# Two cache passes of a hybrid decoder step: row loads asked for earlier in one, a fifth row buffer in the other

## The chip, the cores and the metric

The kernel runs on one core of a Trainium2 chip. The metric is the device time of one execution in microseconds (us), and the time of a version is the median of its runs. A profile is of one execution. TensorE is PE in its rows (PEld is its weight load), VectorE is DVE, ScalarE is ACT, GpSimd is POOL and SyncE is SP; SPq, ACTq and POOLq are the DMA issues of those engines. The core has 16 DMA engines that all queues share.

## The reference, cut to what matters

The program is one layer step of a hybrid autoregressive decoder: a prompt of 512 tokens and 8 sample sequences of 8 new tokens each, the latter over 4096 cached positions in pages of 128 rows. Three groups of heads share one input projection; the change lies in the sample side of the last two of them:

```
o_dsa: score = indexer(q, idx cache); keep the best 256 keys of each query (6 q / 2 kv heads)
o_cmp: attention over 32-row blocks that an MLP has compressed; its probabilities rank the 64-row blocks
o_slc: attention over the best 16 of the 64-row blocks (slc K and V of the NSA cache)
o_win: attention over the last 512 positions (window state)
nsa  = g0 * o_cmp + g1 * o_slc + g2 * o_win
```

Both `o_slc` and `o_dsa` are computed as dense passes over the whole cache with a mask for the keys that were not chosen. Each of them reads K and V of 2 heads, 8 sequences, 4096 positions, 128 wide, in float32: 64 MB, 2 MB at a time.

## The kernel before, in words

The kernel is a row of blocks, each with its own program for every engine. A block ends when all engines have come to its end; only then does the next begin. Around the change the blocks are: `compress` (TensorE-heavy), `cmp_sample` (the compressed attention), the pass `slc` over the selected blocks, the pass `dsa` over the top-k keys (called the top-k pass here), the pass `win` over the window state, and then the prompt's blocks.

The three passes are one function, `stream`. A cache pass has 32 steps: 4 groups of 2 sequences, and in each 8 pieces of 512 positions. A step needs 4 pages of each of its 2 sequences: 8 DMAs of 128 rows x 512 floats, 256 KB each, so 2 MB a step. They go into one of the row buffers: `second`, the two halves of `region`, and `rows3` (the profile calls the last one `kept_rows`). Buffer 0 is `kept_second`, buffers 1 and 2 are `kept_region`.

TensorE's program of a pass is, for each step: turn the keys of step n (`turn`, L1643), turn the probabilities of step n-1 (L1666), score step n (L1653 and L1656), and multiply the values of step n-1 (`values`, L1682), which signals `v_used`. ScalarE copies the turned keys (L1756) and does the exponentials, VectorE adds the bias with the running maximum (L1821), copies the probabilities (L1829) and adds up (L1839). In the first five steps of `slc` VectorE also does the last of the top-k search (L978, L980), and one mask (L2042).

The loads are asked for by SyncE's program, in order. In `stream` it waits for the `v_used` of the step that had the same buffer before, and then issues the 8 DMAs of the next step (L914), each with a page number that was read into a register ahead (L905). Steps below `ready` are not issued there, since an earlier block did: step 0 of `slc` in `compress`, step 1 in `cmp_sample`, behind two small loads of new values (L934) and ahead of the bias `bias_nsa` (L1013, 4 DMAs of 24 rows of 16 KB). At the end of its own steps a pass calls `ahead`: `slc` there loads half of the bias of the next pass, `kept_bias_lo` (4 DMAs of 24 rows of 8 KB and 4 of 24 rows of 32 bytes; ACT's queue brings the other half in `dsa`), and the first three steps of `dsa`; `dsa` loads the bias of `win`, its new values, and the first three of the four row sets of `win` (L1912). Each of these waits in `free(n)` until the buffer n has been used for the last time by the pass that still runs.

In `slc` VectorE first waits for `bias_nsa`, adds a mask to its end (L1581), makes the scores of the new tokens (L1804) and their maximum (L1806); ScalarE needs this for the exponentials of the new tokens (L1782), behind four copies of keys.

Of the kernel before, what the change touches and what calls it, by code (L numbers as in the profile page):

```python
# [16 lines left out]
F32 = mybir.dt.float32  # L17
# [7 lines left out]
P = 128  # L25
# [4 lines left out]
PAST = 4096  # L30
# [888 lines left out]
AHEAD = 3  # L919


def step_rows(sp, nc, io, kept, tag, cache, col, n, free):

    g, c = divmod(n, NCH)
    free(n)
    pages = page_numbers(nc, io, kept.paired, g * (2 * NPG) + c * (2 * PPC), 2 * PPC)
    for b in range(2):
        to = kept.rows[n % 4].rearrange("p (b m c) -> p b m c", b=2, m=PPC)[:, b]
        load_pages(sp, pages[b * PPC:(b + 1) * PPC], to, cache, col, 4 * DH, kept.arrived[tag][n % 4][b])


def new_values(sp, io, kept, tag, col):
# [573 lines left out]
def stream(nc, io, kept, tag, *, cache, col, heads, per, q, k_new, select=None, dropped_keys=None, bias=None,  # L1506
# [9 lines left out]
    width = heads * DH  # L1516
    items = per * heads
    acc_w = DH
    SLOTS = 4
    per_bank = CH // acc_w  # L1520
    banks = groups // per_bank
    with ExitStack() as ctx:
# [41 lines left out]

        def slot(g, c):

            return (c % SLOTS, g * (nch // SLOTS) + c // SLOTS + 1) if nch > 1 else (g % SLOTS, g // SLOTS + 1)

        def parity(g, c):
            return c % 2 if nch > 1 else g % 2  # L1570
# [12 lines left out]
        @block.sync  # L1583
        def _(sp):
            def rows_of(g):

                for c in range(nch):
                    n = c + g * nch
                    i, _ = slot(g, c)
                    if state is None and c % 2 == 0 and n + 1 >= ready:  # L1590

                        pages = page_numbers(nc, io, kept.paired, g * (2 * NPG) + c * (2 * PPC), 4 * PPC)
                    if n < ready:
                        continue
                    for b in range(per):

                        sp.wait_ge(v_used, n * per + b + 1)
                        if state is not None:
                            sp.dma_start(rows[i][:, b], state[g * per + b].rearrange("(m p) c -> p m c", p=P)).then_inc(rows_in[i][b], 64)
                        else:  # L1600
                            first = (c % 2 * per + b) * PPC
                            load_pages(sp, pages[first:first + PPC], rows[i][:, b], cache, col, 2 * width, rows_in[i][b])

            each_group(sp, rows_of)
            for to, first in extra:
                sp.wait_ge(zeroed, 3)
                load_bias(sp, io, to, first, KEYS - to.shape[1], later_in)

            def free(n):

                sp.wait_ge(v_used, SLOTS * per + (groups * nch - 4 + n + 1) * per)

            if ahead is not None:
                ahead(sp, free)
# [12 lines left out]
        def _(pe):  # L1627
            pe.nop().then_inc(k_turned, SLOTS * items)
            pe.nop().then_inc(scored, KTS)
            pe.nop().then_inc(probs_turned, 2)  # L1630
            pe.nop().then_inc(v_used, SLOTS * per)

            def turn(g, c, j):
                n = c + g * nch
# [155 lines left out]
        def _(dve):  # L1790
# [33 lines left out]
            def copy_probs(g, c):  # L1824
                n = c + g * nch
                dve.wait_ge(probs_turned, n + 3)

                dve.wait_ge(v_used, (n - 1 + SLOTS) * per)
                dve.tensor_copy(pT[parity(g, c)][:], qp[:]).then_inc(pT_copied, 1)  # L1829

            def add_up(g, c):
                n = c + g * nch
                dve.wait_ge(v_used, (n + 1 + SLOTS) * per)
                to = acc[:, bass.ds(g, 1), :].rearrange("p o c -> p (o c)")
                new = pv[parity(g, c)][:, 0:acc_w]
                dve.wait_ge(acc_done, n + 2)
                dve.wait_ge(shrunk, n + 1)
                by = shrink[:, bass.ds(g, 1), c + 1:c + 2].rearrange("p o k -> p (o k)")
                dve.scalar_tensor_tensor(to, to, by, new, ALU.mult, ALU.add).then_inc(acc_done, 1)  # L1839
# [79 lines left out]
def cmp_sample(nc, io, kept):  # L1919


    with ExitStack() as ctx:
# [17 lines left out]
        @block.sync  # L1940
        def _(sp):
            new_values(sp, io, kept, "slc", NSA_VS)
            new_values(sp, io, kept, "dsa", DSA_V)
            step_rows(sp, nc, io, kept, "slc", io.nsa_cache, 512, 1, lambda n: None)
            sp.wait_ge(bias_zeroed, 1)
            load_bias(sp, io, kept.bias_nsa, 6, 0, kept.bias_nsa_in)

        @block.gpsimd
        def _(pool):
# [72 lines left out]
def slc_sample(nc, io, kept):  # L2022
# [13 lines left out]
    def spare(dve, n):  # L2036
# [3 lines left out]
        elif n == SEARCH_LATE + 1:  # L2040
# [1 line left out]
            dve.tensor_scalar(kept.drop[:], kept.scores[:], GONE / 2, NEG, ALU.is_gt, ALU.mult)  # L2042

    stream(nc, io, kept, "slc", cache=io.nsa_cache, col=512, heads=2, per=2, q=kept.q_nsa, k_new=kept.k_slc,
           ready=2, select=kept.sel_e, dropped_keys=keys, bias=lambda lo, hi: kept.bias_nsa[:, lo:hi], bias_in=(kept.bias_nsa_in, 64),
           zero=kept.bias_lo, ahead=ahead, spare=spare, head0=10, gate=1, add=True)


# [851 lines left out]
def program(nc, io):  # L2900
    with ExitStack() as ctx:
# [29 lines left out]
        with ExitStack() as sample_ctx:  # L2931
# [7 lines left out]
            kept.w1_values_in, kept.pe_in, kept.top_step = sample.sem("w1_values_in"), sample.sem("pe_in"), sample.sem("top_step")  # L2939
            kept.rows = [kept.second[:]] + [kept.region[:, i * 4096:(i + 1) * 4096] for i in range(2)]  # L2940
            for tag in ("slc", "dsa", "win"):
                kept.arrived[tag] = [[sample.sem(f"{tag}_in{i}_{b}") for b in range(2)] for i in range(4)]
            kept.arrived["cmp"] = [sample.sem(f"cmp_in{i}") for i in range(CMP_RING)]
            with ExitStack() as cmp_ctx:
                compressing = Scope(nc, cmp_ctx, "kept")
# [14 lines left out]
            with nc.sbuf_tensor("bias_nsa", [P, KEYS], F32) as bias_nsa:  # L2960
                kept.bias_nsa = bias_nsa[:]
                cmp_sample(nc, io, kept)
                slc_sample(nc, io, kept)
            with nc.sbuf_tensor("bias_hi", [P, PAST // 2], F32) as kept.bias_hi:
                dsa_sample(nc, io, kept)
            win_sample(nc, io, kept)
        kept.oT = kept.region[:].rearrange("p (h t) -> p h t", t=SEQ)
        with ExitStack() as prompt_ctx:
# [70 lines left out]
```

## Time and profile before

| what | value |
|---|---|
| median of 3 runs | 2450.25 us (2448.75 to 2451.13) |
| the profiled execution's own time | 2450.47 us |
| its span, first to last instruction | 2448.7 us |
| mean granted TensorE clock | 0.961 |
| PE busy | 2270.8 us, 93% |
| DVE / ACT / POOL busy | 38% / 35% / 21% |
| DMA | 523.15 MB, mean 214 GB/s |

The span is 1.8 us shorter than the execution's own time, which holds what lies around the first and the last instruction. The busy share of PE is one over the whole kernel; in the passes that the change touches, the share of the DMA engines is as high as PE's, so that the rows below take the passes by themselves. A granted clock of 1.00 is 2.4 GHz, one of 0.50 is 1.2 GHz.

### The profile page before, as it was taken

How to read it: one execution, taken by the hardware profiler on the slowest of the kernel's cores; microseconds unless marked ns; L12 is line 12 of the kernel's file. 1: busy time of each engine (PE TensorE's matmuls, PEld its weight loads, DVE VectorE, ACT ScalarE, POOL GpSimd, SP SyncE). 2: the span in 40 equal slices, each digit the busy share in tenths (PEclk: the TensorE clock that was granted, in tenths of full speed). 3: DMA queues.
4: the chain of work that ended last, by engine and by line, in shares of the span. 5: the costliest groups of instructions: out<-in, count | busy, mean ns of one | idle time of the engine just before them, and what ended most of it. 6: DMA issues, size and time to landing. Idle time of an engine off the chain costs nothing. (4 is left out here: it accounts for less than half of the span.)

```text
span 2448.7 us, 46127 instructions
## 1 busy us (share of the span) xinstructions
PE 2270.8 (93%) x16622; PEld 1753.7 (72%) x16625; DVE 941.7 (38%) x1657; ACT 856.8 (35%) x1913; POOL 506.9 (21%) x405
## 2 busy tenths in 40 slices
PE   6999999999999999988999998888799867999996
PEld 4887777777777777775999998555455544777885
DVE  5111111212111111125488885533233348876123
ACT  4001332223222232212344443355455466662100
POOL 5433222222222222223100000000000000444332
PEclk7999999999999999999999999899899976999998
DMA  4755676767676767568566664899999976002423
GB/s 148 216 176 200 236 257 212 264 224 261 228 242 230 265 225 265 191 165 208 177 195 194 196 196 136 276 373 382 278 381 380 313 230 201 1 1 95 128 79 120
DMA packets 321699, 523.15 MB, mean 214 GB/s; under 512 B 36981, under 2 KB 128518, under 8 KB 319638
## 3 DMA queue, kind: packets, MB, share of 16 engines
q1 hardware_dynamic: 300642, 487.56, 60.1%
q10 hardware_dynamic: 16416, 23.13, 2.9%
q0 software_dynamic: 4416, 9.52, 1.2%
q8 instruction: 133, 2.18, 0.4%
q14 instruction: 92, 0.75, 0.1%
HBM read 497.83 MB, written 44.00 MB: 221 GB/s over the span
## 5 line engine op out<-in xcount | busy, mean ns | idle before, releaser
L549 POOL TENSOR_TENSOR proj_w_lo<-kept_region,proj_w_hi 128x1024 fp32r<-128x1024 f32 (+1 forms) x120 | 282.5, 2355 | 720.8 <-DVE proj_w_hi L800 720.8
L580 PE MATMUL proj_acc<-proj_w_hi,h_hi 128*128 128x512 f32 (+1 forms) x952 | 389.8, 409 | 0.0
L582 PE MATMUL proj_acc<-proj_w_lo,h_hi 128*128 128x512 f32 (+1 forms) x952 | 368.9, 388 | 0.0
L581 PE MATMUL proj_acc<-proj_w_hi,h_lo 128*128 128x512 f32 (+1 forms) x952 | 368.2, 387 | 0.0
L752 ACT COPY proj_kT<-proj_tp 128x512 f32<-128x512 f32 x256 | 150.3, 587 | 402.8 <-PE proj_tp L641 348.2
L800 DVE CAST proj_w_hi<-kept_region 128x1024 fp32r<-128x1024 f32 (+1 forms) x120 | 86.9, 726 | 382.8 <-PE proj_acc L584 380.1
L580 PEld LDWEIGHTS proj_acc<-proj_w_hi,h_hi 128*128 128x128 f32 x952 | 179.1, 188 | 60.3 <-issue 31.7
L582 PEld LDWEIGHTS proj_acc<-proj_w_lo,h_hi 128*128 128x128 f32 x952 | 178.7, 188 | 37.5
L581 PEld LDWEIGHTS proj_acc<-proj_w_hi,h_lo 128*128 128x128 f32 x952 | 179.6, 189 | 27.6
L1206 ACT COPY cmp_xT<-cmp_tp 128x512 f32<-128x512 f32 x260 | 139.0, 588 | 159.7 <-PE cmp_tp L1119 159.7
L641 PE MATMUL proj_tp<-kept_consts,kept_region 128*128 128x128 f32 x1024 | 153.7, 272 | 0.1
L641 PEld LDWEIGHTS proj_tp<-kept_consts,kept_region 128*128 128x128 f32 x1024 | 126.1, 140 | 35.9 <-ACT proj_kT L752 6.0
L1119 PE MATMUL cmp_tp<-kept_consts,kept_second 128*128 128x128 f32 x1040 | 138.5, 278 | 6.2 <-DMA kept_second<-in_cache_nsa_kv_dram 3.7
L978 DVE MAX8 kept_top<-kept_scores 64x8 f32<-64x4104 f32 x32 | 141.5, 4423 | 0.5
L980 DVE MATCH_REPLACE8 kept_scores<-kept_top,kept_scores 64x4104 f32<-64x4104 f32 x32 | 141.1, 4408 | 0.0
L1119 PEld LDWEIGHTS cmp_tp<-kept_consts,kept_second 128*128 128x128 f32 x1040 | 119.9, 143 | 8.4 <-DMA kept_second<-in_cache_nsa_kv_dram 6.2
L1177 PE MATMUL cmp_hp<-cmp_xT,kept_region 128*128 128x128 f32 x1024 | 125.8, 277 | 0.0
L1177 PE MATMUL cmp_hp<-cmp_xT,kept_w_values 128*128 128x128 f32 x1024 | 123.8, 275 | 0.0
L1177 PEld LDWEIGHTS cmp_hp<-cmp_xT,kept_region 128*128 128x128 f32 x1024 | 120.5, 193 | 0.0
L1177 PEld LDWEIGHTS cmp_hp<-cmp_xT,kept_w_values 128*128 128x128 f32 x1024 | 118.9, 192 | 0.0
L708 ACT COPY proj_out<-proj_acc 128x512 f32<-128x512 f32 (+1 forms) x60 | 34.6, 578 | 209.5 <-PE proj_acc L582 200.2
L2736 POOL TENSOR_TENSOR fin_w_lo<-kept_second,fin_w_hi 128x1024 fp32r<-128x1024 f32 x32 | 79.5, 2486 | 110.7 <-DVE fin_w_hi L2837 110.7
(459 smaller groups left out, 3640.3 us busy)
## 6 DMA issues: line engine op xcount, KB each, us to landing
kept_region<-in_cache_sb_kv_dram SPq DMA_DIRECT2D x256, 256.0 KB, 4.9
kept_second<-in_cache_sb_kv_dram SPq DMA_DIRECT2D x256, 256.0 KB
kept_second<-in_cache_nsa_kv_dram SPq DMA_DIRECT2D x512, 128.0 KB, 2.4
kept_region<-in_w_in_dram SPq DMA_DIRECT2D x112, 512.0 KB, 6.1
kept_region<-in_cache_nsa_kv_dram SPq DMA_DIRECT2D x128, 256.0 KB, 5.0
kept_region<-in_cache_dsa_kv_dram SPq DMA_DIRECT2D x128, 256.0 KB, 4.7
kept_second<-in_cache_nsa_kv_dram SPq DMA_DIRECT2D x64, 256.0 KB, 4.9
kept_rows<-in_cache_nsa_kv_dram SPq DMA_DIRECT2D x64, 256.0 KB, 5.2
```

The source lines that it names most:

```text
L549: pool.tensor_tensor(w_lo[p % SPLIT][:, :, here], w[p % RAW][:, :, here], w_hi[p % SPLIT][:, :, here], ALU.subtract).then_inc(lo_made, 1)
L580: pe.matmul(to, h_hi[:, kk, r], hi[:, k], start=first, stop=False)
L581: pe.matmul(to, h_lo[:, kk, r], hi[:, k], start=False, stop=False)
L582: last = pe.matmul(to, h_hi[:, kk, r], lo[:, k], start=False, stop=final)
L641: last = pe.transpose(tp[:, x:x + P], k_rows[:, b, p, h * DH:(h + 1) * DH], kept.ident)
L752: act.copy(kT[:, h % 2, 2 * pair:2 * pair + 2, :], tp[:].rearrange("p (b k) -> p b k", b=2)).then_inc(kT_copied, 1)
L800: dve.tensor_copy(w_hi[p % SPLIT][:, :, here], w[p % RAW][:, :, here]).then_inc(hi_made, 1)
L978: dve.max(kept.top8[:], kept.scores[:]).then_inc(kept.top_step, 1)
L980: dve.match_replace(kept.scores[:], kept.top8[:], kept.scores[:], GONE).then_inc(kept.top_step, 1)
L1119: last = pe.transpose(tp[n % 2 * 2 + a][:, p * P:(p + 1) * P], rows[i][:, p, a, :], kept.ident)
L1177: last = pe.matmul(hp[e][:, a, :], w1(2 * e + a, r), xT[:, 2 * e + a, r, :], start=(r == 0), stop=(r == CMPB - 1))
L1206: act.copy(xT[:, a, :, to], tp[n % 2 * 2 + own][:].rearrange("p (c r) -> p r c", r=CMPB)).then_inc(x_copied, 1)
```

## The change

Three things are done.

1. `ready` of `slc` becomes 4, and `cmp_sample`'s SyncE program issues steps 2 and 3 of `slc`, behind `bias_nsa`. Each is preceded by its own reading of 8 page numbers.
2. The pass `dsa` has five row buffers, the fifth being `rows4`, which lives only during this pass. Buffer numbers, arrival semaphores and the waits for a buffer follow from `slots(tag)`; `slc` and `win` keep four.
3. The semaphore `v_used` starts at zero and no longer at 4 buffers' worth, with the waits rewritten to match; a wait for a buffer that nobody has used yet is left out.

```
+def slots(tag):
+    return 5 if tag == "dsa" else 4

 step_rows:
-        to = kept.rows[n % 4]...
+        to = kept.rows[n % slots(tag)]...

 stream:
-    SLOTS = 4
+    SLOTS = slots(tag)
-            return (c % SLOTS, g * (nch // SLOTS) + c // SLOTS + 1) if nch > 1 else (g % SLOTS, g // SLOTS + 1)
+            n = g * nch + c
+            return n % SLOTS, n // SLOTS + 1
-                        sp.wait_ge(v_used, n * per + b + 1)
+                        if n >= SLOTS:
+                            sp.wait_ge(v_used, (n - SLOTS + 1) * per)
 free(n):
-                sp.wait_ge(v_used, SLOTS * per + (groups * nch - 4 + n + 1) * per)
+                sp.wait_ge(v_used, max(m + 1 for m in range(groups * nch) if m % SLOTS == n) * per)
-            pe.nop().then_inc(v_used, SLOTS * per)
-                dve.wait_ge(v_used, (n - 1 + SLOTS) * per)
+                if n >= 2:
+                    dve.wait_ge(v_used, (n - 1) * per)
-                dve.wait_ge(v_used, (n + 1 + SLOTS) * per)
+                dve.wait_ge(v_used, (n + 1) * per)

 cmp_sample, SyncE:
             load_bias(sp, io, kept.bias_nsa, 6, 0, kept.bias_nsa_in)
+            for n in (2, 3):
+                step_rows(sp, nc, io, kept, "slc", io.nsa_cache, 512, n, lambda n: None)

 slc_sample:
-           ready=2, select=kept.sel_e, ...
+           ready=4, select=kept.sel_e, ...

 program:
-            with nc.sbuf_tensor("bias_hi", [P, PAST // 2], F32) as kept.bias_hi:
+            with nc.sbuf_tensor("bias_hi", [P, PAST // 2], F32) as kept.bias_hi, nc.sbuf_tensor("rows4", [P, 4096], F32) as rows4:
+                kept.rows.append(rows4[:])
                 dsa_sample(nc, io, kept)
+                kept.rows.pop()
```

SyncE's program at the end of `cmp_sample` and the start of `slc`, before (an ISA row prepares the page's address, a TENSOR_LOAD reads page numbers; the two branches are the end of the block and the start of the next):

```order
L914 DMA kept_region<-in_cache_nsa_kv_dram 128x512
L1013 DMA bias_nsa<-token_lines 24x4104 x4
L1922 UNCONDITIONAL_BRANCH
L1583 UNCONDITIONAL_BRANCH
L905 TENSOR_LOAD kept_paired
L914 ISA
L914 DMA kept_region<-in_cache_nsa_kv_dram 128x512
...
L914 DMA kept_rows3<-in_cache_nsa_kv_dram 128x512
L905 TENSOR_LOAD kept_paired
```

The same place of the changed kernel:

```order
L914 DMA kept_region<-in_cache_nsa_kv_dram 128x512
L1017 DMA bias_nsa<-token_lines 24x4104 x4
L905 TENSOR_LOAD kept_paired
L914 ISA
L914 DMA kept_region<-in_cache_nsa_kv_dram 128x512
...
L905 TENSOR_LOAD kept_paired
L914 ISA
L914 DMA kept_rows3<-in_cache_nsa_kv_dram 128x512
...
L1928 UNCONDITIONAL_BRANCH
L1588 UNCONDITIONAL_BRANCH
L905 TENSOR_LOAD kept_paired
```

All 16 loads of steps 2 and 3, with one more reading of page numbers, now stand ahead of the branch that ends `cmp_sample`.

SyncE's program at the end of the top-k pass, before:

```order
L914 DMA kept_rows3<-in_cache_dsa_kv_dram 128x512
L1013 DMA kept_bias_win<-token_lines 24x520 x4
L934 DMA kept_v_new0<-proj 8x8x256
L1912 DMA kept_second<-in_state_nsa_win_dram 128x4x512 x2
L1912 DMA kept_region<-in_state_nsa_win_dram 128x4x512 x4
L1522 UNCONDITIONAL_BRANCH
```

And of the changed kernel:

```order
L914 DMA kept_region<-in_cache_dsa_kv_dram 128x512
L1017 DMA kept_bias_win<-token_lines 24x520 x4
L938 DMA kept_v_new0<-proj 8x8x256
L1918 DMA kept_second<-in_state_nsa_win_dram 128x4x512 x2
L1918 DMA kept_region<-in_state_nsa_win_dram 128x4x512 x4
L1526 UNCONDITIONAL_BRANCH
```

The loads stand in the same order; what differs is which buffer the last step (31) uses, 1 in place of 3, and so which steps the three row sets of `win` wait for: buffer 0 is last used by step 30 (before: 28), buffer 1 by step 31 (before: 29), buffer 2 by step 27 (before: 30).

## Rows read from the trace of the kernel before

**Rows 1.** Compressed attention, `slc`, `dsa`: busy PE PEld DVE ACT POOL, clock, DMA share, GB/s.

```profile
1524.80:1543.40 18.60, 11.30 (x76) 10.35 (x76) 6.23 (x31) 2.23 (x9) 3.52 (x1) 0.52 0.75 198
1543.40:1743.20 199.80, 167.88 (x2028) 109.10 (x2028) 80.79 (x154) 97.49 (x237) 2.28 (x2) 0.97 1.00 349
1743.90:1936.70 192.80, 169.88 (x2028) 109.12 (x2028) 61.74 (x147) 97.32 (x237) 2.75 (x3) 0.97 1.00 353
```

**Rows 2.** Waits for DMA in the two passes: us in total, times, longest.

```profile
PE slc_tp L1643 <- DMA kept_second<-in_cache_nsa_kv_dram: 0.8, 1, 0.8
PEld dsa_tp L1643 <- DMA kept_second<-in_cache_dsa_kv_dram: 0.3, 1, 0.3
```

**Rows 3.** SyncE's issues, `cmp_sample` into `slc`: start, us, engine, line, tiles.

```profile
1524.79 0.69 SPq L934 DMA_DIRECT2D kept_v_new<-proj  x2
1526.47 4.53 SPq L914 DMA_DIRECT2D kept_region<-in_cache_nsa_kv_dram  x8
1531.05 2.10 SPq L1013 DMA_DIRECT2D bias_nsa<-token_lines  x4
1544.79 4.10 SPq L914 DMA_DIRECT2D kept_region<-in_cache_nsa_kv_dram  x8
1549.08 4.73 SPq L914 DMA_DIRECT2D kept_rows<-in_cache_nsa_kv_dram  x8
1559.30 4.01 SPq L914 DMA_DIRECT2D kept_second<-in_cache_nsa_kv_dram  x8
```

**Rows 4.** Timeline at the block boundary and the first steps of `slc`.

```profile
1541.19 1.52 DVE L2017 COPY kept_oTs<-ca_ov 128x24 f32<-128x24 f32 x16 [6.86 <-PE ca_ov L1974]
1543.45 0.52 POOL L1620 MEMSET slc_prob_new<- 128x512 f32 x1 [15.13 <-POOLq L157]
1546.38 0.17 DVE L1581 TENSOR_TENSOR bias_nsa<-bias_nsa,kept_consts 128x8 f32<-128x8 f32 x1 [3.67 <-DMA bias_nsa<-token_lines]
1549.74 0.30 ACT L1782 ACTIVATE slc_prob_new<-slc_log_new,slc_nmax 128x8 f32<-128x8 f32 x1
1559.02 1.09 PE L1643 MATMUL slc_tp<-kept_consts,kept_region 128*128 128x128 f32 x8
```

**Rows 5.** SyncE's issues at the end of `slc`.

```profile
1713.78 4.03 SPq L914 DMA_DIRECT2D kept_rows<-in_cache_nsa_kv_dram  x8
1717.86 4.29 SPq L1013 DMA_DIRECT2D kept_bias_lo<-token_lines  x8
1723.21 5.58 SPq L914 DMA_DIRECT2D kept_second<-in_cache_dsa_kv_dram  x8
1729.53 11.63 SPq L914 DMA_DIRECT2D kept_region<-in_cache_dsa_kv_dram  x16
```

**Rows 6.** Step 31's last load, issue to landing (us at the end); PE behind it.

```profile
kept_rows<-in_cache_nsa_kv_dram SPq DMA_DIRECT2D x1, 256.0 KB, 12.2
...
1729.69 2.45 PE L1643 MATMUL slc_tp<-kept_consts,kept_rows 128*128 128x128 f32 x12 [4.44 <-DMA kept_rows<-in_cache_nsa_kv_dram]
```

**Rows 7.** Load of an ordinary step (1708 to 1713) to landing; two issues in `dsa`, 16 steps apart.

```profile
kept_region<-in_cache_nsa_kv_dram SPq DMA_DIRECT2D x8, 256.0 KB, 4.8
...
1784.62 4.76 SPq L914 DMA_DIRECT2D kept_second<-in_cache_dsa_kv_dram  x8
...
1873.33 4.33 SPq L914 DMA_DIRECT2D kept_second<-in_cache_dsa_kv_dram  x8
```

**Rows 8.** End of `dsa` and start of `win`; a 1 MB load elsewhere, to landing.

```profile
1919.36 0.99 SPq L1912 DMA_DIRECT2D kept_second<-in_state_nsa_win_dram  x2
...
1927.79 1.06 PE L1682 MATMUL dsa_pv<-kept_region,dsa_pT 128*32 128x128 f32 x32
...
1938.19 3.73 PE L1643 MATMUL win_tp<-kept_consts,kept_second 128*128 128x128 f32 x16 [0.17 <-ACT L1744]
...
kept_second<-in_x_prompt_dram SPq DMA_DIRECT2D x1, 1024.0 KB, 4.7
norm_x<-in_x_prompt_dram SPq DMA_DIRECT2D x4, 1024.0 KB, 9.0
```

More of the change, by code:

```diff
@@ L927, in step_rows @@
     for b in range(2):
-        to = kept.rows[n % 4].rearrange("p (b m c) -> p b m c", b=2, m=PPC)[:, b]
-        load_pages(sp, pages[b * PPC:(b + 1) * PPC], to, cache, col, 4 * DH, kept.arrived[tag][n % 4][b])
+        to = kept.rows[n % slots(tag)].rearrange("p (b m c) -> p b m c", b=2, m=PPC)[:, b]
+        load_pages(sp, pages[b * PPC:(b + 1) * PPC], to, cache, col, 4 * DH, kept.arrived[tag][n % slots(tag)][b])
 def new_values(sp, io, kept, tag, col):
@@ L2044, in slc_sample @@
     stream(nc, io, kept, "slc", cache=io.nsa_cache, col=512, heads=2, per=2, q=kept.q_nsa, k_new=kept.k_slc,
-           ready=2, select=kept.sel_e, dropped_keys=keys, bias=lambda lo, hi: kept.bias_nsa[:, lo:hi], bias_in=(kept.bias_nsa_in, 64),
+           ready=4, select=kept.sel_e, dropped_keys=keys, bias=lambda lo, hi: kept.bias_nsa[:, lo:hi], bias_in=(kept.bias_nsa_in, 64),
            zero=kept.bias_lo, ahead=ahead, spare=spare, head0=10, gate=1, add=True)
@@ L2941, in program @@
             for tag in ("slc", "dsa", "win"):
-                kept.arrived[tag] = [[sample.sem(f"{tag}_in{i}_{b}") for b in range(2)] for i in range(4)]
+                kept.arrived[tag] = [[sample.sem(f"{tag}_in{i}_{b}") for b in range(2)] for i in range(slots(tag))]
             kept.arrived["cmp"] = [sample.sem(f"cmp_in{i}") for i in range(CMP_RING)]
```

## The prediction

> **What bounds the kernel now.** I read the split by stretches first, since the change touches three blocks only [rows 1]. The compressed attention is 18.6 us in which the DMA engines are 75% busy at 198 GB/s; the two cache passes take 199.8 and 192.8 us, with PE busy 84% and 88% of the time and the DMA engines at a share of 1.00. The reader is to see that PE and DMA look equally full there, so that the shares alone don't say which of the two sets the pace. The view of waits does: in the whole of `slc` PE waits for rows once for 0.8 us [rows 2] and once for 4.44 us [rows 6], and in `dsa` the weight loads wait once for 0.3 us [rows 2]. That is all. The steps of `dsa` come at (1873.33 - 1784.62) / 16 = 5.54 us [rows 7], with the rows there in time; PE's own chain with ACT and DVE sets it. So a cache pass is bound by PE, with a DMA system just fast enough: 2.1 MB in 5.54 us are 378 GB/s. In `slc` too, the DMA system has no part in the pace of the early steps: PE turns the keys of step 2 at 1559.02, with no wait marked in the row [rows 4], and step 3 comes a step later. Their loads had been issued from 1544.79 and from 1549.08 to 1553.81 [rows 3].
>
> **Steps 2 and 3 of `slc` asked for earlier: the gain.** No wait stands before these two steps, so none goes. Step 4 uses buffer 0 and is issued when step 0 has been multiplied, at 1559.30 [rows 3]; this isn't moved, nor is anything behind it. The one small wait in the pass, 0.8 us on `kept_second`, is for a step whose load waits for `v_used` in the same way as before. I keep it; the bounds are 0 and -0.8 us.
>
> **The same, its cost.** SyncE's issues are part of `cmp_sample` now, and the block can't end before they are done. Before, SyncE was through at 1531.05 + 2.10 = 1533.15 [rows 3], while VectorE ended the block at 1541.19 + 1.52 = 1542.71, and `slc` began at 1543.45, 0.74 us later [rows 4]. SyncE had some 9.5 us of cover. Into it go two readings of pages and 16 DMAs. The first reading takes what lies between 1524.79 + 0.69 and 1526.47, 1.0 us [rows 3]; for the second I take 0.7, the gap from 1723.21 + 5.58 to 1729.53 [rows 5]. For the DMAs the rows give two prices:
> - on free queues 4.01 to 4.10 us for 8 [rows 3]: SyncE ends at 1533.15 + 1.0 + 4.0 + 0.7 + 4.0 = 1542.85, and `slc` begins 0.2 us later than it did (1542.85 + 0.74 - 1543.45 = 0.14, rounded up);
> - behind a bias load and on queues that are backed up, which is the state they will be in, 5.58 us for the first 8 and 11.63 for 16 with a gap of 0.7 within, so 5.5 each [rows 5]. Then SyncE ends at 1533.15 + 1.0 + 5.6 + 0.7 + 5.5 = 1545.95, and `slc` begins 3.2 us later. The bias here is twice as large as the one of rows 5 (rows of 16 KB, there of 8 KB), so I set the upper bound at 4.5.
>
> I take 2.5 us, between the two and nearer to the row that is like it, since part of the 16 will be issued after the bias has drained. PE's chain begins that much later, and nothing later in the kernel takes it back: passes and prompt are one chain of blocks.
>
> **The bias behind which they queue.** `bias_nsa` is itself waited for: DVE goes on at 1546.38, after 3.67 us of idleness that its landing ended [rows 4]. The result is needed by ACT for L1782 at 1549.74; from L1581 on DVE needs some 0.5 us, so there are 2.9 us of cover, and with a block that begins 2.5 us later, 5.4. What the 4 MB behind the bias do to its landing is not shown. The nearest row is the last row load of step 31: with a bias load issued directly behind it, it took 12.2 us [rows 6] where the loads of a step before took 4.8 [rows 7]. So something queued behind can stretch a load, by up to 7.4 us; from below, it is 0. If the bias were stretched by that, it would cost 7.4 - 5.4 = 2.0 us. I take 0: the bias consists of few long rows, it was the bias that slowed the others in that row, and the DMA engines are at 0.75 in this stretch, so there is room beside it.
>
> By a rule of the Trainium skill (DMA: Bandwidth & Descriptors, section Queues, rings and completion order) each DMA engine takes the descriptors of a queue in ring order, so that loads issued behind the bias don't come before it. By that rule the bias lands as before and the term is 0; by the row of 12.2 us, a landing does depend on what is queued behind it, and the term is up to 2.0. The sum above needs only the rows.
>
> **The fifth buffer in `dsa`.** Step n+5 and not n+4 is issued when step n has been multiplied, so that each load has 5.54 us more until it is needed. There is one wait of 0.3 us to take [rows 2]; I take it off. Steps 3 and 4 are both issued at the start of the pass, with the second half of the bias on ACT's queue; neither that half nor step 4 is needed before four steps of 5.54 us have passed, some 22 us. The pace stays PE's 5.54 us.
>
> **The price of the fifth buffer at the end.** The row sets of `win` now wait for other steps. The first went out at 1919.36, when step 28 had been multiplied; now it waits for step 30, which ends at 1927.79 + 1.06 = 1928.85 [rows 8]. It is 2 MB and is needed by PE at 1938.19, 9.3 us later [rows 8]. The DMA engines are idle by then, since step 31 has been issued 5.5 us earlier than before. A load of 1 MB takes 4.7 us on free queues and its fellow another 1.05 / 0.378 = 2.8 us, together 7.5: 1.8 us to spare. The dearest 1 MB load of the trace, 9.0 us, would give 11.8 and a wait of 2.5. I take 0. The second set follows when step 31 has been multiplied and lands a further 5.5 us after the first (2 MB at 378 GB/s), by 1941.9; PE needs it no earlier than a step after the first, 1938.19 + 5.54 = 1943.7. So it goes on, set for set.
>
> **The rewritten waits** (a NOP of PE, one wait of SyncE for each sequence) change no moment at which anything is released: 0.
>
> **Sum.** 2450.47 + 2.5 (later start of `slc`) + 0 (bias) - 0.3 (one wait in `dsa`) + 0 (`win`) = 2452.7 us, made against the profiled execution. That one is 0.2 us above the median of the runs, so I expect 2452.5 as the median. The bounds of the terms alone: 0.2 - 0.8 - 0.3 = -0.9 below, and 4.5 + 2.5 = +7.0 above (the late bias and the late block share one cover and don't add up). The likeliest case by itself is 2449.5 to 2455.
>
> **Rivals.**
> 1. *The long wait at the end of `slc` goes.* If the 4.44 us [rows 6] are a backlog that the pass has carried since its first steps, then loads issued 10 us earlier shrink it, and with it the half-speed matmuls behind it: the 12 transposes there take 2.45 us. That would be -4.4 - 1 - 0.3 + 2.5 = -3.2, or -5.7 with a free start: 2447.3 to 2444.8. For it speaks the DMA share of 1.00 over the pass. Against it: the loads of the step before took the usual 4.8 us [rows 7], and only the last load before the bias 12.2; a backlog would show in both. 8%.
> 2. *Slower, by SyncE in the block.* The mechanism of my own largest term, at its end: the queues are so full behind `bias_nsa` that SyncE stands in its DMAs until the bias and most of step 2 have landed. The point from which it decides is SyncE's end, 1542.7; beyond 1547.4 it costs more than can be told from no change. With step 3's loads standing until step 2's 2 MB have landed behind the bias, 5.5 us beyond the free-start case of 1542.85, this gives 5 to 8 us: 2455.5 to 2458.5. 13%.
> 3. *Slower, by `win`.* The first row set lands after 1938.19 plus the shift: up to 2.5 us more, 2455.2. For it: one buffer's cover of 19 us has become 9.3. Against it: idle DMA engines. 7%.
> 4. *Nothing happens*: SyncE keeps to its cover and no wait goes, within 0.5 us of before: 2450.5. 20%.
>
> **How the numbers follow.** About 0.2% (4.9 us) is what a measurement of this kernel can tell from no change, so 2445.4 to 2455.2 counts as the same. My forecast has 52%, nearly all of it in that band; so have case 4 and most of case 3. Slower by over 0.2%: case 2 with its 13%, and 3% from the upper end of the others. Faster by over 0.2%: the farther half of case 1, and unknown gains, 7% in all. The range holds the bounds of the terms and reaches somewhat to case 1: 2447 to 2457.
>
> **What the profile after would show.** SyncE's 16 loads of steps 2 and 3 between 1534 and some 1545, and the first instruction of `slc` (POOL's MEMSET) near 1546 and not at 1543.45; if it is at 1543.5, the largest term is wrong. DVE's L1581 directly at the start, with no wait for the bias, or one that ends before ACT's L1782 would have begun. Again one wait of some 4.4 us for `kept_rows` in the last step of `slc`; if it is gone, case 1 holds. No wait for DMA in `dsa`, steps at 5.54 us. The first row set of `win` issued right behind step 30, and no wait of PE at the first `win_tp`. The prediction fails if one of the long waits for DMA has gone, or if PE has one that wasn't there.

## The result and the profile after

The changed kernel takes 2455.49 us (median of 12 runs, 2452.56 to 2462.68), the kernel before 2448.27 us beside it (12 runs, 2446.07 to 2452.72): a ratio of 1.0032, 95% interval 1.0024 to 1.0041, so 0.3% slower, some 7 us. Beside the last experiments the changed kernel was run again: 2454.33 us (11 runs), ratio 1.0026 (1.0017 to 1.0035).

The profiled execution of the changed kernel took 2452.56 us with a span of 2450.8, at a mean granted clock of 0.960. It was the quickest of its twelve. Its three stretches, which answer to [rows 1] (us, busy PE PEld DVE ACT POOL, clock, DMA share, GB/s):

```profile
1524.70:1550.80 26.10, 11.63 (x76) 10.69 (x76) 6.24 (x31) 2.23 (x9) 3.52 (x1) 0.51 0.89 214
1550.80:1747.50 196.70, 167.26 (x2028) 109.44 (x2028) 80.82 (x154) 97.38 (x237) 2.28 (x2) 0.97 0.97 342
1747.50:1939.50 192.00, 168.86 (x2028) 109.38 (x2028) 61.81 (x147) 97.19 (x237) 2.74 (x3) 0.97 0.96 346
```

The compressed attention has become 7.5 us longer with the same busy times; `slc` is 3.8 us shorter and `dsa` 0.8. SyncE's issues of the first of these stretches, which answer to [rows 3]:

```profile
1526.38 4.68 SPq L914 DMA_DIRECT2D kept_region<-in_cache_nsa_kv_dram  x8
1531.10 2.14 SPq L1017 DMA_DIRECT2D bias_nsa<-token_lines  x4
1534.25 4.30 SPq L914 DMA_DIRECT2D kept_region<-in_cache_nsa_kv_dram  x8
1539.29 10.67 SPq L914 DMA_DIRECT2D kept_rows<-in_cache_nsa_kv_dram  x8
```

Step 2's eight loads go out in 4.30 us, step 3's take 10.67. In a narrower window the second load of step 3 stands alone:

```profile
1540.15 3.27 SPq L914 DMA_DIRECT2D kept_rows<-in_cache_nsa_kv_dram  x1
```

Most single issues of this stretch take 0.33 us; this one stood 3.27. What the block and the next one did meanwhile, to be held against [rows 4]:

```profile
1541.42 1.53 DVE L2025 COPY kept_oTs<-ca_ov 128x24 f32<-128x24 f32 x16 [6.86 <-PE ca_ov L1982]
1550.83 0.53 POOL L1626 MEMSET slc_prob_new<- 128x512 f32 x1 [22.60 <-POOLq L157]
1551.06 0.17 DVE L1586 TENSOR_TENSOR bias_nsa<-bias_nsa,kept_consts 128x8 f32<-128x8 f32 x1 [8.11 <-PEq L157]
```

VectorE was through at 1542.95, SyncE at 1549.96, and `slc` begins at 1550.83 instead of 1543.45. L1586 no longer waits for the bias. The step that waits at the end of `slc`, against [rows 6]:

```profile
1733.31 2.91 PE L1648 MATMUL slc_tp<-kept_consts,kept_rows 128*128 128x128 f32 x12 [2.03 <-DMA kept_rows<-in_cache_nsa_kv_dram]
```

2.03 us in place of 4.44. And the end of `dsa`, against [rows 8]:

```profile
1933.44 5.07 SPq L1918 DMA_DIRECT2D kept_region<-in_state_nsa_win_dram  x4
...
1937.40 0.16 DVE L1586 TENSOR_TENSOR kept_bias_win<-kept_bias_win,kept_consts 128x8 f32<-128x8 f32 x1
1939.56 3.76 SPq L1605 DMA_DIRECT2D kept_rows<-in_state_nsa_win_dram  x2
1939.57 0.52 POOL L1626 MEMSET win_prob_new<- 128x512 f32 x1 [189.28 <-POOLq L157]
...
1941.00 3.73 PE L1648 MATMUL win_tp<-kept_consts,kept_second 128*128 128x128 f32 x16 [0.33 <-ACT L1749]
```

SyncE stands in the last of these loads too: it is through at 1938.51, VectorE at 1937.56, so the block ends 2.01 us behind VectorE, where a block that nothing else holds ends 0.8 us behind it. PE waits for no row at the start of `win`.

Taken apart by POOL's first instruction of each block (the last column runs from the start of `win` to the end of the span; us):

| execution | compressed attention | slc | dsa | the rest |
|---|---|---|---|---|
| before | 18.64 | 200.52 | 192.79 | 511.94 |
| changed | 26.12 | 196.72 | 192.02 | 511.23 |
| changed, a second profile | 25.46 | 195.83 | 192.67 | 516.83 |

The rest of one and the same kernel differs by 5.6 us between two executions, more than any single term except the first. A window over its first part shows what goes with it: the clock (the column before the last two).

```profile
1940.00:2100.00 160.00, 121.05 (x748) 82.27 (x749) 101.54 (x231) 99.19 (x219) 8.58 (x22) 0.77 0.66 210
```

```profile
1940.00:2100.00 160.00, 119.09 (x696) 81.17 (x696) 97.47 (x213) 95.34 (x209) 5.92 (x15) 0.75 0.66 210
```

The first is the changed kernel, the second its second profile, which has done less of every engine's work in the same 160 us at a lower granted clock; that the clock is the cause of all 5.6 us isn't shown. The moment at which the compressed attention begins varies as well, from 1522.13 to 1527.50 us over all profiles of this document, though none of the edits lies ahead of it. So the difference of two spans can't be read as the effect of the change; stages must be compared, and medians.

### The profile page after: what moved, and what is told of

Same layout as the page of the kernel before. It is cut to its first block and busy times, and to the rows that moved or that the text cites. A ratio compares the mean times of both kernels' runs of the same rounds, so it can differ in the third digit from the quotient of the medians.

```text
span 2450.8 us, 46122 instructions
## 1 busy us (share of the span) xinstructions
PE 2268.5 (93%) x16622; PEld 1752.8 (72%) x16625; DVE 943.3 (38%) x1657; ACT 856.4 (35%) x1913; POOL 506.4 (21%) x405
```

## The experiments

"Same" below means that the 95% interval of the ratio to the kernel before contains 1. The experiments were run in three groups of four (those with steps 2 and 3 or the fifth buffer alone, the bias on ScalarE's queue and step 2 alone; those of the bias; the rest), each beside its own runs of the kernel before: 2448.63, 2448.87 and 2448.72 us.

**Steps 2 and 3 early, `dsa` with four buffers.**

```
 def slots(tag):
-    return 5 if tag == "dsa" else 4
+    return 4
```

> Only steps 2 and 3 of slc are asked for in cmp_sample; dsa has four buffers. Theory A (SyncE stands in its DMAs behind bias_nsa and so holds cmp_sample open): SyncE ends near 1550, slc starts near 1550.8 (+7.4 us against 1543.45), and nearly all of the 7.2 us that the change costs is here, about +6 (the fifth buffer's end of dsa, +1.2, is gone): 2453.5 to 2455. Rival B (the fifth buffer costs the time, by SyncE's last loads of dsa and what follows in win): this kernel is within 2 us of the kernel before although slc starts late, 2448 to 2450. A further reading within A: the 4.44 us wait for kept_rows at the end of slc is about 2 us, as in the changed kernel, if it follows from how far the loads run ahead.

Measured: 2453.3 us (11 runs), ratio 1.0022 (1.0013 to 1.0032). The first eight early loads take 4.19 us, the second 9.87; the compressed attention lasts 25.72 us, `slc` 197.37. The wait for step 31's rows is 2.38 us, near the 2 that theory A asked for. The loss belongs to the early loads; rival B falls.

**The fifth buffer alone.**

```
-            for n in (2, 3):
-                step_rows(sp, nc, io, kept, "slc", ...)
-           ready=4, ...
+           ready=2, ...
```

> Only the fifth buffer of dsa; slc is asked for as before. Theory A: slc starts at 1543.5 as before, the 4.44 us wait is as before, dsa's end costs about 1.2 us because SyncE stands in the last two loads of win's row sets, less 0.3 for the wait in dsa: 2449 to 2450. Rival B (the fifth buffer carries the loss): 2453 to 2456.

Measured: 2447.79 us (11 runs), ratio 0.9990 (0.9981 to 0.9999), 1.2 us below what theory A had. The compressed attention lasts 18.59 us, `dsa` 192.04. The fifth buffer costs nothing that the time shows.

The wait for step 31's rows did not stay at 4.44 us, as I had expected for a pass whose loads are asked for as before:

```profile
1729.65 2.91 PE L1648 MATMUL slc_tp<-kept_consts,kept_rows 128*128 128x128 f32 x12 [2.79 <-DMA kept_rows<-in_cache_nsa_kv_dram]
```

`slc` lasted 197.82 us, 2.7 less than in the profile of the kernel before, though it is started and fed as there. Only the rewritten waits differ in it, and no run has these by themselves. So either they are worth something, or two profiles of the same pass differ by up to 3 us; shorter passes below must be held against 197.8 as well as 200.5.

**The bias on ScalarE's queue.**

```
 cmp_sample, SyncE:
-            sp.wait_ge(bias_zeroed, 1)
-            load_bias(sp, io, kept.bias_nsa, 6, 0, kept.bias_nsa_in)
 cmp_sample, ScalarE, behind its exponentials:
+            act.wait_ge(bias_zeroed, 1)
+            load_bias(act, io, kept.bias_nsa, 6, 0, kept.bias_nsa_in)
```

> The changed kernel, but bias_nsa is issued by ScalarE's queue in cmp_sample, behind its exponentials; SyncE's 16 loads of steps 2 and 3 are as in the changed kernel but with nothing of the bias ahead of them in their queue. Theory A1 (they stand because their own queue is full behind the slow rows of the bias): single issues are 0.3 to 0.6 us again, SyncE ends by 1541 to 1543, slc starts at 1543.5 to 1544.5, and the loss of 7.4 us there is gone; the time is 2447 to 2450. Rival A2 (they stand because 4 MB more are asked of the DMA engines in that stretch, whatever the queue): SyncE still ends after 1547, slc starts at 1548 or later, 2453 to 2456.

Measured: 2458.49 us (8 runs), ratio 1.0041 (1.0027 to 1.0054). SyncE's issues, and within them one load of step 2:

```profile
1525.90 16.19 SPq L914 DMA_DIRECT2D kept_region<-in_cache_nsa_kv_dram  x13
1542.84 5.17 SPq L914 DMA_DIRECT2D kept_rows<-in_cache_nsa_kv_dram  x8
```

```profile
1534.62 3.77 SPq L914 DMA_DIRECT2D kept_region<-in_cache_nsa_kv_dram  x1
```

Now SyncE stands in step 2 and not in step 3. The compressed attention still lasts 26.74 us, and the median is 2.5 us above rival A2's range. My theory A1 falls: SyncE stands without any load of the bias ahead in its own queue. The bias slows the row loads from another queue too; ScalarE issues it earlier in the block than SyncE did (3.6 us after its start and not 6.4).

**Step 2 alone.**

```
-            for n in (2, 3):
+            for n in (2,):
-           ready=4, ...
+           ready=3, ...
```

> The changed kernel, but only step 2 is asked for in cmp_sample, behind bias_nsa; step 3 is the first load of slc. Theory A: the first 8 loads took 4.3 us, so SyncE ends at 1538.6, VectorE ends the block as before, slc starts at 1543.5; the 7.4 us are gone and what is left is +1.2 at the end of dsa and what a shorter wait at the end of slc gives back: 2447 to 2450. Rival B (the early loads cost by what they do to the landing of bias_nsa or to the engines): step 2 alone costs about half, 2452 and more, with a wait for bias_nsa at the start of slc.

Measured: 2447.47 us (11 runs), ratio 1.0003 (0.9990 to 1.0015): same. The block closes at its old place, with the bias landing later than before and still hidden:

```profile
1534.38 4.39 SPq L914 DMA_DIRECT2D kept_region<-in_cache_nsa_kv_dram  x8
...
1541.52 1.52 DVE L2025 COPY kept_oTs<-ca_ov 128x24 f32<-128x24 f32 x16 [6.86 <-PE ca_ov L1982]
1543.78 0.53 POOL L1626 MEMSET slc_prob_new<- 128x512 f32 x1 [15.20 <-POOLq L157]
1548.88 0.17 DVE L1586 TENSOR_TENSOR bias_nsa<-bias_nsa,kept_consts 128x8 f32<-128x8 f32 x1 [5.84 <-DMA bias_nsa<-token_lines]
...
1549.91 0.30 ACT L1787 ACTIVATE slc_prob_new<-slc_log_new,slc_nmax 128x8 f32<-128x8 f32 x1
```

The 7 us are gone with eight loads fewer. L1586 comes 2.5 us later than in [rows 4]; ScalarE's exponential 0.2 us later, straight behind its copies. `slc` lasted 194.68 us and the wait for step 31 was 0.56 us.

**The long rows left out.** Only the first 64 columns of `bias_nsa` are loaded, so `slc` lacks the bias of most keys.

```
-            load_bias(sp, io, kept.bias_nsa, 6, 0, kept.bias_nsa_in)
+            load_bias(sp, io, kept.bias_nsa[:, 0:64], 6, 0, kept.bias_nsa_in)
```

> The changed kernel with nearly all of bias_nsa left out: its 4 loads bring only the first 64 of 4104 columns (so slc adds no bias for most keys). It is a measurement of the long rows. Theory A (SyncE stands once some 2.1 to 2.6 MB of its own queue are outstanding, and they are because the bias's rows of 16 KB keep 12 of 16 DMA engines for about 10 us): SyncE is bound by its own issuing, ends near 1543.5, slc starts near 1544.4 instead of 1550.8, about 6 us are back, 2448.5 to 2450.5. Rival (16 loads more than before are too many for the queue whatever is ahead of them): SyncE still ends after 1547 and slc starts after 1548, 2453 to 2456.

Measured: 2447.23 us (12 runs), ratio 0.9992 (0.9983 to 1.0001).

```profile
1536.24 4.72 SPq L914 DMA_DIRECT2D kept_region<-in_cache_nsa_kv_dram  x8
1541.70 4.27 SPq L914 DMA_DIRECT2D kept_rows<-in_cache_nsa_kv_dram  x8
...
1546.84 0.52 POOL L1626 MEMSET slc_prob_new<- 128x512 f32 x1 [16.84 <-POOLq L157]
```

All 16 loads go at nearly their free price, and the median is 1.3 us below theory A's range. This execution was 1.8 us late on entering the block (1526.49 against 1524.71 in the changed kernel), so that the block's length is what to compare: 20.35 us, 1.7 longer than before, where the changed kernel's is 7.5 longer. Without the bias SyncE doesn't stand.

**The bias in short pieces.** Its 4 loads become 8 (here for `bias_nsa`; the wait for them counts twice as many):

```
+        here, rows = (x.rearrange("p (b a k) -> p a b k", a=2, b=4) for x in (here, rows))
+        for a in range(2):
+            eng.dma_start(here[:, a], rows[:, a]).then_inc(sem, 16)
```

> The changed kernel with bias_nsa in pieces of 2052 bytes: 8 loads of 24 x 4 x 513 instead of 4 of 24 x 4104; the result is the same. Theory A: packets of 2 KB spread over all 16 engines at about 0.09 us each, so the 1.6 MB take 4 to 5 us and not 10; SyncE has 4 issues more (1.9 us) and ends near 1545.5, slc starts near 1546.3, 2450 to 2452. Rival (the long time belongs to the 24 partitions or to the source, not to the form of the rows): the packets are short but the bias still takes about 10 us, and slc starts near 1550.8 or later, 2455 or more.

Measured: 2453.17 us (11 runs), ratio 1.0025 (1.0013 to 1.0037); compressed attention 26.19 us. A window while the bias alone is on its way, first of the kernel before, then of this one (DMA share and GB/s at the end):

```profile
1537.00:1543.00 6.00, 4.15 (x20) 4.03 (x19) 1.52 (x16) 0.00 (x0) 0.00 (x0) 0.50 0.74 156
```

```profile
1534.50:1538.50 4.00, 4.00 (x20) 4.00 (x21) 0.00 (x0) 0.00 (x0) 0.00 (x0) 0.50 0.82 150
```

The rate stays at 150 GB/s. By the trace's packets, 12 packets of 16 KB are under way at any moment of the first window, 1.27 us each; here it is 12 to 13 packets of 2052 bytes, and one takes 0.17 us, where one of a page row of 2048 bytes takes 0.09. So the pieces neither spread the load further nor move at the rate of the page rows: my theory A on the form of the rows falls, and the length of the rows isn't the reason. That only 12 to 13 packets are under way can be a part of it, since the edit left that as it was. What does slow this load (its 24 partitions, its source) stays open.

The length of this kernel's block says little on the stand, for it has a cause of its own. The eight issues of the bias took

```profile
1530.17 6.97 SPq L1025 DMA_DIRECT2D bias_nsa<-token_lines  x8
```

where the four of the changed kernel took 2.14 us; I had allowed 1.9 us for four more. Of the row loads only one stood, for 2.12 us.

**The bias last.**

```
-            sp.wait_ge(bias_zeroed, 1)
-            load_bias(sp, io, kept.bias_nsa, 6, 0, kept.bias_nsa_in)
             for n in (2, 3):
                 step_rows(sp, nc, io, kept, "slc", ...)
+            sp.wait_ge(bias_zeroed, 1)
+            load_bias(sp, io, kept.bias_nsa, 6, 0, kept.bias_nsa_in)
```

> The changed kernel, but SyncE issues steps 2 and 3 ahead of bias_nsa. Theory A: no 16 KB row is ahead of the loads, so they go at 378 GB/s, SyncE ends near 1543.6, slc starts near 1544.4; the bias lands some 10 us later, near 1552.5, VectorE waits for it and ScalarE's exponentials of the new tokens come 2 to 3 us late: 2450.5 to 2453. Rival (the count of loads alone holds SyncE): slc starts after 1548 and the bias is late besides, 2456 or more.

Measured: 2461.94 us (5 runs), ratio 1.0048 (1.0035 to 1.0061), the slowest.

```profile
1525.39 10.61 SPq L914 DMA_DIRECT2D kept_region<-in_cache_nsa_kv_dram  x16
1536.74 4.05 SPq L914 DMA_DIRECT2D kept_rows<-in_cache_nsa_kv_dram  x8
1540.85 1.67 SPq L1017 DMA_DIRECT2D bias_nsa<-token_lines  x4
1543.49 0.52 POOL L1626 MEMSET slc_prob_new<- 128x512 f32 x1 [16.24 <-POOLq L157]
1557.90 0.17 DVE L1586 TENSOR_TENSOR bias_nsa<-bias_nsa,kept_consts 128x8 f32<-128x8 f32 x1 [16.27 <-DMA bias_nsa<-token_lines]
...
1559.91 1.12 PE L1706 MATMUL slc_qp<-kept_consts,slc_prob_new 128*128 128x128 f32 x4 [9.36 <-ACT slc_prob_new L1787]
```

None of the loads of steps 2 and 3 takes over 0.51 us, with 24 loads of rows one behind the other, and the block is 19.76 us long. But the bias lands 5 us later than I expected, PE waits 9.36 us for what follows from it, and `slc` lasts 208.81 us: the median is 9 us above theory A's range. The term "bias", 0 in the change, is dear in this order.

**The kernel before with all of the passes' bias in pieces.** The edit is that of the short pieces, for both halves of `dsa`'s bias too.

> The kernel before, with bias_nsa and both halves of the top-k pass's bias in pieces of 2 KB (twice as many loads, each 24 x 4 x 513 or 24 x 2 x 512); the result is the same. Theory C (the wait of 2 to 4.4 us for step 31's rows at the end of slc is the long rows of the bias issued behind them): step 31 lands in 5 to 7 us instead of 12, the wait is under 1 us, slc starts at 1543.5 without a wait for bias_nsa, 2443.5 to 2446. Rival (the wait is a backlog that the pass has carried, since its steps move data at the rate at which the DMA engines can): the wait stays at 2 to 4.4 us, and the time within 1.5 us of the kernel before.

Measured: 2459.17 us (5 runs), ratio 1.0044 (1.0031 to 1.0057). The wait for step 31's rows was 4.02 us, as before: theory C falls, the rival's first half holds. The other half, a time within 1.5 us of the kernel before, doesn't come. The loss lies in `dsa`, whose length went to 197.57 us, and it begins at its start:

```profile
1745.28 5.24 ACTq L1021 DMA_DIRECT2D bias_hi<-token_lines  x8
```

ScalarE is held 5.24 us by eight issues there (four take 3.03 us in the kernel before and 1.73 in the changed one), ahead of its copies. That is at most 2.2 us of the 4.8 by which `dsa` is longer; the granted clock of the pass was lower too, 0.94 against 0.97, and how the rest divides isn't shown.

**Step 2 early, and the row sets of `win` in another order.**

The edit of step 2 alone, and besides:

```
-        for g in range(AHEAD):
+        for g in (2, 0, 1):
             free(g)
```

> The kernel with only step 2 asked for early and the fifth buffer in dsa, and in addition the row sets of win are issued in the order 2, 0, 1 (set 2's buffer is free after step 27, set 0's after step 30, set 1's after step 31). Theory A: SyncE is through before VectorE at the end of dsa (its last load no longer stands for 3 us), so the block ends 1.2 us earlier and PE has no wait at win's first keys; slc starts at its old place and lasts 195 us instead of 200.5: 2444 to 2447, the quickest version. Rival D (what the passes gain is given back in the prompt's blocks by the granted clock): win starts 6 to 8 us earlier than before, but the time from there to the end is 3 to 6 us longer than 511.9 us, and the median is within 2 us of the kernel before.

Measured: 2448.53 us (11 runs), ratio 0.9999 (0.9988 to 1.0009): same, and not the 2444 to 2447 of theory A.

```profile
1926.71 1.17 SPq L1918 DMA_DIRECT2D kept_region<-in_state_nsa_win_dram  x2
...
1930.21 0.15 DVE L1586 TENSOR_TENSOR kept_bias_win<-kept_bias_win,kept_consts 128x8 f32<-128x8 f32 x1
1931.18 0.39 SPq L1605 DMA_DIRECT2D kept_rows<-in_state_nsa_win_dram  x1
1931.20 0.53 POOL L1626 MEMSET win_prob_new<- 128x512 f32 x1 [187.46 <-POOLq L157]
```

SyncE no longer stands, and the block closes 0.84 us behind VectorE. `slc` lasted 195.46 and `dsa` 190.21 us, together 7.6 less than before; the rest lasted 516.80 us, 4.9 more. That is rival D's picture, but it isn't shown that the one causes the other: the changed kernel's own two profiles differ as much in the rest.

**A late start by itself.** In the kernel before, GpSimd fills a tile 11 times behind its zeroing of the bias, and so holds the block.

```
+            for i in range(HOLD):          # HOLD = 11
+                pool.wait_ge(bias_zeroed, i + 1)
+                pool.memset(kept.bias_lo[:], 0.0).then_inc(bias_zeroed, 1)
```

> The kernel before, with the compressed attention's block held open by GpSimd: 11 fills of a tile (1.8 us each) behind its zeroing of bias_nsa, each waiting for the one before; no load is asked for earlier. slc starts near 1550, as in the changed kernel. If a later start passes into the time one for one, this gives +6 to +7: 2454 to 2456. What slc lasts tells the rest apart: 200 us means that the changed kernel's 196.7 us come from its early loads (theory A); 196 to 197 us means that they come from the late start itself, since the loads have had time to land.

Measured: 2455.87 us (7 runs), ratio 1.0025 (1.0014 to 1.0036), for a block of 24.86 us, 6.2 longer. `slc` lasted 197.12 us and waited 1.51 us for step 31. A late start alone is enough for a loss like the changed kernel's. `slc` is 3.4 us shorter here than in the profile of the kernel before, where the changed kernel has 3.8; of this the fifth buffer alone, with neither early loads nor a late start, shows 2.7. `dsa` lasted 195.62 us in this execution, the slowest of its seven, at a granted clock of 0.94.

**Half of the loads in `dsa`.** From step 8 on only the keys of each row are loaded; the values are what the buffer held.

```
+                            part = width if tag == "dsa" and n >= 8 else 2 * width
+                            load_pages(sp, ..., rows[i][:, b, :, 0:part], cache, col, part, rows_in[i][b])
```

> The changed kernel, but from step 8 on dsa loads only the keys of its rows (1 KB of each 2 KB row; the values are those that the buffer held), so 1 MB a step. If the top-k pass is bound by PE with ACT and DVE, as the prediction has it, the steps stay at 5.5 us and dsa at 192 us: 2454 to 2456, as the changed kernel. If the DMA system sets its pace (2 MB in 5.54 us are just about what it moves at its best), the steps come quicker, 5.0 us or less, and dsa is 10 us or more shorter.

Measured: 2452.43 us (7 runs), ratio 1.0020 (1.0009 to 1.0032), `dsa` 193.28 us. Two issues, 15 steps apart:

```profile
1790.75 4.31 SPq L914 DMA_DIRECT2D kept_second<-in_cache_dsa_kv_dram  x8
...
1873.46 5.46 SPq L914 DMA_DIRECT2D kept_second<-in_cache_dsa_kv_dram  x8
```

82.71 / 15 = 5.51 us a step with 1 MB, against 5.54 with 2 MB [rows 7]: PE with ACT and DVE sets the pace.

**The changed kernel again.**

> The changed kernel once more, beside the others of this group, for a second profile and a median on the same chip: 2453 to 2457. slc again starts 7 us late, with single loads of step 3 that stand over 1 us. If the profiled execution is one of the slower kind (2460 and more), theory D has the difference in the granted clock of win and the prompt's blocks; the rival has it in a longer stand of SyncE.

Measured: 2454.33 us (11 runs, 2451.09 to 2460.62). The profiled execution's span is 4.8 us longer than the first one's, with a compressed attention 0.7 us shorter: the difference is in the rest, where theory D had it, though this execution was not one of 2460 and more.

The stages of the profiles on which the account below rests (us; the last column is the wait for step 31's rows in `slc`):

| execution | compressed attention | slc | dsa | the rest | wait |
|---|---|---|---|---|---|
| before | 18.64 | 200.52 | 192.79 | 511.94 | 4.44 |
| fifth buffer alone | 18.59 | 197.82 | 192.04 | 512.05 | 2.79 |
| steps 2 and 3 alone | 25.72 | 197.37 | 192.56 | 511.10 | 2.38 |
| changed | 26.12 | 196.72 | 192.02 | 511.23 | 2.03 |
| bias in pieces, four buffers | 18.58 | 200.26 | 197.57 | 514.09 | 4.02 |
| late start by itself | 24.86 | 197.12 | 195.62 | 516.59 | 1.51 |
| step 2 alone | 18.73 | 194.68 | 190.95 | 515.39 | 0.56 |

## Why the prediction was right and wrong

The median lies in the range (2447 to 2457) and 3.0 us above the forecast. The direction is the forecast's, the size is not: 2.3 us more than the kernel before were forecast, 7.2 measured, just over the +7.0 that the bounds of the terms allowed. That the time lies so well within the range is in part luck, since the kernel before took 2448.27 us beside it and not the 2450.25 from which I had started. I gave "same" 77% and "slower" 16%, and it is slower by 0.3%. What happened is rival 2, to which I gave 13% and 5 to 8 us.

- *What bounds the passes*: right for `dsa`, by the half loads (5.51 against 5.54 us a step). In `slc`, where no half loads were tried, the steps from the eighth on come 5.54 us apart as well in the traces of both kernels, but for one gap of 6.5 us in the kernel before, which holds its 0.8 us wait.
- *Later start of `slc`*: the step that failed is this term of the sum, 2.5 us with a bound of 4.5; it measured 7.5 (26.12 - 18.64), 6.8 in the second profile and 7.1 with the early steps alone. My upper price for eight loads was 5.5 us, from loads behind half as large a bias [rows 5]. The first eight were cheaper (4.30) and the second eight twice as dear (10.67). One price for every eight loads was the wrong form: a load costs 0.33 us until it stands, and in the changed kernel it stood when the bias and nine loads had been issued ahead of it. What makes it stand isn't settled. Counting packets in the trace: when the 3.27 us issue began, 1,122 of the 2,272 packets of rows and bias that SyncE had asked for hadn't ended; in the kernel with the bias on ScalarE's queue it was 969 when SyncE first stood for long (1.88 us) and about 1,030 at the 3.77 us issue. With the long rows left out, or the bias last, it was never more than 868, and nothing of steps 2 and 3 took over 0.96 us. But a number of pending packets is no limit by itself: with the bias in short pieces loads went out in 0.33 us with 1,454 pending, and in the changed kernel the number rose to 1,335 while SyncE stood. How the packets lie on the 16 DMA engines I haven't counted. What the runs show is that the long stands come with the bias on its way, and not with step 2's eight loads alone behind it. In the changed kernel 7.9 MB of rows and bias were asked for in this stretch, and the DMA engines moved 199 GB/s of it from 1536 to 1541 us and 131 from 1541 to 1546, at shares of 1.02 and 0.96.
- *The cover*: right. SyncE may take until VectorE's end; step 2 alone stays inside, and the block lasts 18.7 us.
- *The bias*: 0, right. Its later landing is hidden (L1586 2.5 us later with step 2 alone, ScalarE 0.2). The reason that I took first was wrong, though. A landing does depend on what is queued behind, as the row on the last load [rows 6] had it: the last packet of the bias ended at 1545.84 us in the kernel before, at 1547.91 with step 2 alone and at 1547.86 in the changed kernel, and its packets took 1.8 us each toward the end instead of 1.27. So the ring order that the prediction cites from the Trainium skill (DMA: Bandwidth & Descriptors, section Queues, rings and completion order) doesn't keep a landing from being stretched by later loads here. It orders one queue on one DMA engine; here 4 packets of step 2's rows were under way beside the bias's 12, long before the bias had ended.
- *Rival 1, 8%*: its outcome came in part, its mechanism isn't shown. In the three profiles with `slc` asked for as before and started at once, step 31 waited 4.44, 4.02 and 2.79 us; in the eleven others 0.32 to 2.38. So a shorter wait goes with an earlier issue or a later start. But no backlog carried through the pass can be seen: the first load of step 31 goes out 0.20 us after its buffer is free in the kernel before, in the changed one and with the fifth buffer or step 2 alone, and 576, 608, 534 and 531 row packets are pending at that moment, with no order that would fit the waits. What sets this wait stays open. The changed kernel's `slc` is 3.8 us shorter in its profile, which kept that execution at +2.1; held against the 197.82 us of the fifth buffer alone it is 1.1.
- *The fifth buffer*: right in size (-0.3 forecast; alone it measures 1 us less, at the edge of the interval). That SyncE's last load stands there too, 1.2 us of block, I had not foreseen; rival 3's late row set didn't come.
- *"Nothing later takes it back"*: right by the medians of the late start alone (6.2 us of block in its profile, ratio 1.0025, which is 6.1 us). By single profiles the shorter `slc` does take some of it back.

In short: +7.5 for the block, -3.8 in `slc`, -0.8 in `dsa`, -0.7 in the rest, and -0.1 on entering, make the 2.1 us of the two profiled spans. The medians differ by 7.2, the profiled execution of the changed kernel being the quickest of its runs. Open is why the two versions with step 2 early and not step 3, whose passes are 7.6 to 7.7 us shorter in their profiles, come out the same in the median. The fifth buffer alone bears on it: its `slc` is already 2.7 us shorter than in the kernel before, with none of its loads asked for earlier, so that much of the 7.7 isn't the early step 2's. The clock of the rest may take another part.

No version is clearly quicker than the kernel before: the fifth buffer alone is 0.1% quicker with an interval that ends at 0.9999, and the changed kernel with step 2 alone is level with it.

## What to carry to other kernels

Loads moved into an earlier block belong to that block: before you price them by the number of instructions, ask what else the DMA engines move while the block is open. Here 16 more loads behind a slow bias made the block some 7 us longer, eight made it 0.1 longer, and 16 with nearly all of the bias left out 1.7. Before you read a wait at the end of a long pass as a property of the kernel, or a shorter one as an effect of a change, look for a second profile in which the pass is started and fed the same: here the wait was 4.44 us in one and 2.79 in another. And profile the same kernel twice before a few microseconds between two spans are read as an effect.

## What the hardware showed unexpectedly

A load of 24 partitions x 16 KB moved at 156 GB/s with a DMA share of 0.74, and no faster in pieces of 2 KB, while page rows of 128 partitions moved at 380 GB/s, as in this window of the changed kernel behind its bias:

```profile
1548.00:1550.50 2.50, 0.00 (x0) 0.00 (x0) 0.00 (x0) 0.00 (x0) 0.00 (x0) 0.50 1.04 380
```

Mixed with row loads it took them along. The same mix moved 199 GB/s at first and then 131 at a share of 0.96, less than either alone; what changed at 1541 us isn't shown.

```profile
1536.00:1541.00 5.00, 5.00 (x25) 5.00 (x25) 0.00 (x0) 0.00 (x0) 0.00 (x0) 0.50 1.02 199
1541.00:1546.00 5.00, 0.39 (x2) 0.27 (x2) 1.53 (x16) 0.00 (x0) 0.00 (x0) 0.50 0.96 131
```

And a DMA issue of an engine is an instruction that can stand: 3.27 and 3.77 us for one, in two kernels, with the engine's program and its block behind it. Its price also depends on the form of the load: four issues of 24 rows of 16 KB took 2.10 us, eight of 96 pieces of 2052 bytes 6.97.
